# Scale vectors and normalisers loaded as rows and turned on TensorE, and the first two weight tiles sent by ScalarE

## The reference

```python
num = einsum('bhts,bhse->bhte', qk, vf) + s_in[..., None] * einsum('bhtd,bhde->bhte', qf, c)
den = sum(qk, -1) + s_in * einsum('bhtd,bhd->bht', qf, n)
h = num / maximum(abs(den), exp(-m_t))[..., None]
c_new = decay[..., None, None] * c + einsum('bhs,bhsd,bhse->bhde', wl, kf, vf)
n_new = decay[..., None] * n + einsum('bhs,bhsd->bhd', wl, kf)
```

## Time and profile before

| | |
|---|---|
| timed runs | 2895.07, 2895.27, 2896.46 us (median 2895.27) |
| profiled execution, its own time | 2887.62 us |
| its span, first to last instruction | 2885.6 us |
| TensorE busy | 2672.1 us (93%) |
| VectorE busy | 1120.3 us (39%) |
| GpSimd busy | 1074.2 us (37%) |
| ScalarE busy | 468.8 us (16%) |
| mean granted clock of TensorE | 0.961 of 2.4 GHz |
| SP's queue q1 | 255164 packets, 174.29 MB |
| ScalarE's queue q10 | 31616 packets, 15.02 MB |

### The profile page before, as it was taken

The page is one execution under the profiler, slowest core; times in us unless marked ns, Lnnn a source line. Parts: engine busy times, 40 slices in busy tenths (PEclk is TensorE's granted clock), DMA queues, the critical chain, the costliest instruction groups (busy, mean ns, idle before and its releaser), DMA issues. The chain is left out here.

```text
span 2885.6 us, 38309 instructions
## 1 busy us (share of the span) xinstructions
PE 2672.1 (93%) x15388; PEld 2605.5 (90%) x15388; DVE 1120.3 (39%) x1949; ACT 468.8 (16%) x1019; POOL 1074.2 (37%) x591
## 2 busy tenths in 40 slices
PE   7989889988999999999977968888899999999997
PEld 7978779888999999999977957788899999999996
DVE  6433343335333333333346326623533333333334
ACT  4222222212000000000013314411200000000002
POOL 1212111344444445445433420014444444455441
PEclk9999999999999999999988968989999999999998
DMA  4564766210111111111112244331111111111111
GB/s 133 148 93 131 138 140 144 70 45 30 44 44 36 44 44 39 41 44 38 42 46 64 86 110 93 85 111 40 33 44 44 38 42 44 44 43 36 44 36 73
DMA packets 287626, 190.65 MB, mean 66 GB/s; under 512 B 68196, under 2 KB 274692, under 8 KB 287516
## 3 DMA queue, kind: packets, MB, share of 16 engines
q1 hardware_dynamic: 255164, 174.29, 23.3%
q10 hardware_dynamic: 31616, 15.02, 2.1%
q0 software_dynamic: 768, 0.27, 0.0%
HBM read 148.74 MB, written 42.34 MB: 66 GB/s over the span
## 5 line engine op out<-in xcount | busy, mean ns | idle before, releaser
L233 PE MATMUL psum<-xh,wh 128*128 128x384 f32 (+1 forms) x2592 | 600.7, 340 | 53.0 <-DVE xl L199 30.2
L233 PE MATMUL psum<-xh,wl 128*128 128x384 f32 (+1 forms) x2592 | 599.6, 340 | 0.0
L233 PE MATMUL psum<-xl,wh 128*128 128x384 f32 (+1 forms) x2592 | 598.0, 339 | 0.0
L542 POOL TENSOR_TENSOR wh<-raw,ones 128x1024 fp32r<-128x1024 f32 x128 | 246.8, 1928 | 835.9 <-PE psum L233 832.7
L233 PEld LDWEIGHTS psum<-xh,wh 128*128 128x128 f32 x2592 | 469.7, 190 | 58.2 <-issue 38.6
L233 PEld LDWEIGHTS psum<-xl,wh 128*128 128x128 f32 x2592 | 470.8, 190 | 0.0
L233 PEld LDWEIGHTS psum<-xh,wl 128*128 128x128 f32 x2592 | 470.0, 189 | 0.0
L661 DVE TENSOR_TENSOR h<-h,psum 128x400 f32<-128x400 f32 (+1 forms) x528 | 262.6, 553 | 299.3 <-PE psum L233 299.3
L544 POOL TENSOR_TENSOR wl<-raw,wh 128x1024 fp32r<-128x1024 f32 x128 | 353.5, 2762 | 10.0
L1304 PE MATMUL psum<-xh,wh 128*128 128x384 f32 (+1 forms) x792 | 277.5, 350 | 7.9 <-POOL xl L1253 3.2
L1304 PE MATMUL psum<-xl,wh 128*128 128x384 f32 (+1 forms) x792 | 272.6, 344 | 0.0
(11 more groups left out here) (200 smaller groups left out, 2621.0 us busy)
## 6 DMA issues: line engine op xcount, KB each, us to landing
raw<-in_w_gate_up SPq DMA_DIRECT2D x88, 512.0 KB, 3.9
raw<-in_w_down SPq DMA_DIRECT2D x44, 512.0 KB, 3.6
raw<-in_a_w_in SPq DMA_DIRECT2D x24, 512.0 KB, 4.7
fr_qkv<-qkv_d SPq DMA_DIRECT2D x36, 256.0 KB, 4.4
qkv_d<-fr_tmp SPq DMA_DIRECT2D x32, 192.0 KB, 2.0
qr_d<-tmp ACTq DMA_DIRECT2D x8, 584.0 KB, 2.8
x_loaded<-og_d SPq DMA_DIRECT2D x8, 584.0 KB, 5.6
hn_d<-fr_hn_turned SPq DMA_DIRECT2D x36, 128.0 KB, 4.0
```

The source lines that it names most:

```text
L233: mm = pe.matmul(psum[:, bank + c, 0:nt], w(k), x[:, k, t0:t0 + nt], start=(k == 0 and n == 0), stop=(k == nk - 1 and n == 2))
L542: pool.tensor_tensor(wh[:, b, :], raw[:, r, :], unit, ALU.mult).then_inc(hi_s, 1)
```

## The change

At the start, ScalarE loads the six scale vectors as 48 rows of 128 elements, and all of `state_n` as 32 more rows, into one tile `grow`. TensorE turns the 80 rows in one transposition, and VectorE copies 48 columns into `gains` and 32 into `n_in`. ScalarE then sends weight tile 1 and the two halves of the gate tile, so that SP's stream begins with seven x tiles and the wait for tile 2.

In the mLSTM, VectorE copies a head's 8 normalisers from `n_in` into column 256 of `CS` in step 8, and after the head copies those of `CS` and `C` into `n_out`. After the last head TensorE turns `n_out` (36 columns), ScalarE copies the result into `n_rows`, and SP stores it as 32 and 4 rows of 128 elements. The loads of `state_n` and the stores of `n_s` and `n_p` in every head are gone, and the counts of the semaphores follow.

```diff
+    grow, _ = at("fr_small_rows", [6 * KD + NB * HA, P], F32, place[0] + 4 * P * 4)
     hnc = sb("hn_loaded", [P, 2, CW])
+    n_in, n_out, n_rows = sb("n_in", [P, NB, HA]), sb("n_out", [P, NB * HA + HA]), sb("n_rows", [NB * HA + HA, P])
...
-                if n >= 2:
-                    sp.wait_ge(w_hi, n - 1)
-                    sp.wait_ge(w_lo, 2 * n - 2)
-                if n == 0:
-                    sp.wait_ge(gz, 1)
-                    for half in range(2):
-                        sp.dma_start(weight_tile(raw[:, 0, :])[:, :, 32 * half:32 * half + HA],
-                                     ga[:, :, HA * half:HA * half + HA]).then_inc(w_ld[0], 16)
-                else:
-                    kind, hd, j = tiles[n]
-                    sp.dma_start(weight_tile(raw[:, n % 2, :]), (wo if kind == "out" else wi)(j)).then_inc(w_ld[n % 2], 16)
+                sp.wait_ge(w_hi, n - 1)
+                sp.wait_ge(w_lo, 2 * n - 2)
+                kind, hd, j = tiles[n]
+                sp.dma_start(weight_tile(raw[:, n % 2, :]), (wo if kind == "out" else wi)(j)).then_inc(w_ld[n % 2], 16)
...
             def load_states(hd):
                 if hd:
-                    sp.wait_ge(cs_st, 32 * hd)
+                    sp.wait_ge(cs_st, 16 * hd)
                 sp.dma_start(CS[:, :, 0:DV], a["state_c"][:, 0, hd].rearrange("b d e -> d b e")).then_inc(cs_ld, 16)
-                with nc.allow_non_contiguous_dma("normaliser columns"):
-                    sp.dma_start(CS[:, :, DV], a["state_n"][:, 0, hd].rearrange("b d -> d b")).then_inc(cs_ld, 16)
 
             def store_states(hd):
                 sp.wait_ge(csu, NB * (hd + 1))
                 sp.dma_start(a["c_s"][:, 0, hd].rearrange("b d e -> d b e"), CS[:, :, 0:DV]).then_inc(cs_st, 16)
-                with nc.allow_non_contiguous_dma("normaliser columns"):
-                    sp.dma_start(a["n_s"][:, 0, hd].rearrange("b d -> d b"), CS[:, :, DV]).then_inc(cs_st, 16)
 
             def store_c(hd):
                 sp.wait_ge(cup, 9 * (hd + 1))
                 sp.dma_start(a["c_p"][0, 0, hd], C[:, hd % 2, 0:DV]).then_inc(c_st, 16)
-                sp.dma_start(a["n_p"][0, 0, hd].rearrange("(d x) -> d x", x=1), C[:, hd % 2, DV:E1]).then_inc(c_st, 16)
...
             for i in CHUNK_X[0]:
                 load_x(i)
-            load_w(1)
-            load_w(0)
             for i in CHUNK_X[1]:
                 load_x(i)
             load_w(2)
...
+                if g == S0 + HG * HA + 1:
+                    sp.wait_ge(nrd, 1)
+                    sp.dma_start(a["n_s"].rearrange("b a h d -> (b a h) d"), n_rows[0:NB * HA, :]).then_inc(n_st, 16)
+                    sp.dma_start(a["n_p"].rearrange("b a h d -> (b a h) d"), n_rows[NB * HA:NB * HA + HA, :]).then_inc(n_st, 16)
...
             for n, g in enumerate((a["norm_mix"][0], a["a_g_head"][0], a["norm_ffn"][0], a["g_kv"],
                                    a["norm_mix"][1], a["norm_ffn"][1])):
-                with nc.allow_non_contiguous_dma("gain columns"):
-                    act.dma_start(gains[:, n, :], g.rearrange("(k p) -> p k", p=P)).then_inc(gl, 16)
+                act.dma_start(grow[KD * n:KD * n + KD, :], g.rearrange("(k p) -> k p", p=P)).then_inc(gl, 16)
+            act.dma_start(grow[6 * KD:6 * KD + NB * HA, :], a["state_n"].rearrange("b a h d -> (b a h) d")).then_inc(gl, 16)
+            act.dma_start(weight_tile(raw[:, 1, :]), wi(tiles[1][2])).then_inc(w_ld[1], 16)
+            act.wait_ge(gz, 1)
+            for half in range(2):
+                act.dma_start(weight_tile(raw[:, 0, :])[:, :, 32 * half:32 * half + HA],
+                              ga[:, :, HA * half:HA * half + HA]).then_inc(w_ld[0], 16)
...
-            act.wait_ge(gl, 96)
             w_split(0)
             x_squares(0)
             act.wait_ge(const, 5)
+            act.wait_ge(gnd, 2)
...
+                if g == S0 + HG * HA:
+                    act.wait_ge(ntd, 1)
+                    act.activation(n_rows[:], psum[0:NB * HA + HA, KB, 0:P], ACT.Copy).then_inc(nrd, 1)
...
-                    pe.wait_ge(cs_ld, 32 * (hd + 1))
+                    pe.wait_ge(cs_ld, 16 * (hd + 1))
+                    pe.wait_ge(ncd, hd + 1)
...
+            pe.wait_ge(gl, 112)
+            pe.transpose(psum[:, UB, 0:6 * KD + NB * HA], grow[:], ident[0:6 * KD + NB * HA, 0:6 * KD + NB * HA]).then_inc(grt, 1)
             turn_x(0)
...
+                if g == S0 + HG * HA:
+                    pe.wait_ge(nco, HA)
+                    pe.wait_ge(hsd, 10 * HA)
+                    pe.transpose(psum[0:NB * HA + HA, KB, 0:P], n_out[:], ident[:]).then_inc(ntd, 1)
...
-            dve.wait_ge(gl, 96)
+            dve.wait_ge(grt, 1)
+            dve.tensor_copy(gains[:].rearrange("p n k -> p (n k)"), psum[:, UB, 0:6 * KD]).then_inc(gnd, 1)
+            dve.tensor_copy(n_in[:].rearrange("p b h -> p (b h)"), psum[:, UB, 6 * KD:6 * KD + NB * HA]).then_inc(gnd, 1)
             place_x(0)
             diag(0)
+            dve.wait_ge(gnd, 2)
             x_low(0, h, 0, 0)
...
+                    if st == 8:
+                        dve.tensor_copy(CS[:, :, DV], n_in[:, :, hd]).then_inc(ncd, 1)
+                    if st == 10:
+                        dve.wait_ge(csu, NB * (hd + 1))
+                        dve.wait_ge(cup, 9 * (hd + 1))
+                        dve.tensor_copy(n_out[:, hd:NB * HA:HA], CS[:, :, DV])
+                        dve.tensor_copy(n_out[:, NB * HA + hd:NB * HA + hd + 1], C[:, hd % 2, DV:E1]).then_inc(nco, 1)
```

More of the change, by code:

```diff
@@ L815, in front @@
     rinv = sem("fr_pool_rinv")
+    grt, gnd, ncd, nco, ntd, nrd, n_st = (sem("fr_" + x) for x in (
+        "small_rows_turned", "small_columns", "n_columns", "n_collected", "n_turned", "n_rows", "n_stored"))
     qmz, vao = sem("fr_q_masked_zeroed"), sem("fr_v_ones_set")
@@ L998, in _ @@
                     sp.wait_ge(hst[1], 16 * 20)
-                    sp.wait_ge(cs_st, 32 * HA)
-                    sp.wait_ge(c_st, 32 * HA)
+                    sp.wait_ge(cs_st, 16 * HA)
+                    sp.wait_ge(c_st, 16 * HA)
                     for j in range(SPILL):
@@ L1008, in _ @@
             sp.wait_ge(meta_st, 16)
+            sp.wait_ge(n_st, 32)
             sp.wait_ge(wcopy, 32)
@@ L1482, in gated @@
                         dve.wait_ge(hst[1], 16 * 20)
-                        dve.wait_ge(cs_st, 32 * HA)
-                        dve.wait_ge(c_st, 32 * HA)
+                        dve.wait_ge(cs_st, 16 * HA)
+                        dve.wait_ge(c_st, 16 * HA)
                 dve.scalar_tensor_tensor(dst, tmp[:, g % 4, 0:nt], gains[:, 1, j:j + 1], hnc[:, k % 2, 0:nt],
@@ L1587, in state @@
                         if hd >= 2:
-                            dve.wait_ge(c_st, 32 * (hd - 1))
+                            dve.wait_ge(c_st, 16 * (hd - 1))
                         dve.tensor_copy(C[:, v, :], psum[:, UB, 0:E1]).then_inc(cup, 1)
```

## The result

The changed kernel takes 2848.4 us (median of four runs, 2842.57 to 2850.56), the kernel before beside it 2895.17 us (2894.71 to 2896.46). The ratio is 0.9835, interval 0.9818 to 0.9852: 46.8 us faster.

What follows compares the result with a forecast made beforehand. TensorE was taken as the bound, so only its waits and slow stretches pay. −35.4 + 1.0 (waits) − 1.0 (start) + 0.4 (transposition) = −35.0 us from 2887.62 gave 2852.6; with 7.65 carried over, 2860.3 us, range 2854 to 2878.

Steps and rivals of the forecast that it cites:

- the head changes: At three changes of head in the mLSTM, stalls behind the 4-byte `n_s` stores would go, gaining 35.4 us before leftover waits.
- `c_s` rivals: At the head changes, `c_s` causes half the stall (about 2878 us, chance 0.11) or all (2894.7 us, chance 0.08).
- residual waits: At the three changes of head, 1.0 us in all of waiting for loads would remain.
- new transposition: At group 66 after the last head, turning 36 collected columns on TensorE would add 0.4 us, bounds 0.3 and 1.0.
- start: At the kernel's start, the split of x would begin at 21.3 us instead of 22.28, gaining 1.0 us.
- The two rivals at the start: ScalarE's queue runs ahead of x, split near 19 us (2858 us, chance 0.04); first weights starve (above 2901 us, chance 0.03).
- After the fourth head the mLSTM steps are over and no long wait is listed, so I count nothing.: Behind the last head's `n_s` store, no stall was counted: 0 us gained there.
- I carry the same difference over.: The timed median of the kernel before lay 7.65 us above its profiled execution; the same was added for the changed kernel.

Runs made afterwards that it cites:

- third profile of before: The kernel before, run again without an edit for a trace beside its timed runs; this trace has a span of 2877.7 us and a shorter stall.
- half of `n_s`: The kernel before with 512 instead of 1024 elements in each head's `n_s` store: 2864.64 us, ratio 0.9932.
- stores only: The kernel before with only the `n_s` and `n_p` stores made as rows after the last head, start and loads as they were: 2845.28 us, ratio 0.9864.
- No `c_s`: The kernel before with the `c_s` store left out, `n_s` still stored as single elements: 2867.85 us, ratio 0.9935.

## Why the prediction was wrong

**Right: the head changes.** The sum took 35.4 us from pitches of line 1329; 35.5 went. The tenth is a match with one trace: in the third profile of before the `qkv` waits are 20.6 us, not 24.6. The cause was right as well: `n_s`, not `c_s`. That the price goes by the element was not in the forecast; half of `n_s` shows it. Both `c_s` rivals are refuted: stores only has the whole gain with `c_s` in place. No `c_s` shows what was right in them: `c_s` sets when the stall begins.

**Right within a fraction: residual waits, new transposition, start.** The 1.0 us for waits left over was about 0 (1.3 us in four waits, all under 0.5). The new transposition shows as no wait: TensorE's instruction at group 66 has no idle time before it. The start's 1.0 us became 0.7 at the split of x and 0.17 at head 0 in this trace, and 1.2 at head 0 in the mean of all. That the first split came at 16.02, near the 15.7 of the forecast, is luck: not the gate tile's landing released it, but the end of ScalarE's own issuing and the table load behind it, which the forecast had put into the wait. The two rivals at the start did not come about: the split of x was neither at 19 us nor late.

**Wrong, first: "After the fourth head the mLSTM steps are over and no long wait is listed, so I count nothing."** The fourth store cost 4 to 5.4 us. From traces: of the 41.7 us at line 233's first matmul, 5.3 come behind the last change of head; leaving out that store alone gives 5.4 in its trace and 4.1 in time. A sign of it stood in the trace of before, in VectorE's waits and not in TensorE's, which the forecast read. The lateness went from h rows to VectorE's gating, from there to GpSimd's and VectorE's splits of the output chunks, and reached TensorE 30 us later as a wait of 1.97 us and a stretch in part at 1.2 GHz.

**Wrong, second: "I carry the same difference over."** The 7.65 us between a profiled execution and a timed median were treated as a constant of the program. In four other groups the kernel before had medians 2 to 4 us below its profiled execution, with ratios of 0.9867 and 0.9861 for the changed one, about 38 to 40 us. So the change is worth some 39 us, near the 40.0 of the two profiles; in the first measurement the kernel before was 10 to 12 us slower than in the other four groups, the changed one only 2 to 5, and the difference went into the 46.8. What made it slower there stays open, since no trace of an execution of 2895 us exists.

Adding up: 36.4 (the changes of head and the 0.9 ahead of and between them) + 5.3 (the fourth store) − 1.6 (from line 233 to the end the profile after is 2252.3 − 2250.7 = 1.6 us longer) = 40.1, the difference of the spans.

## What to carry to other kernels

Price a slow transfer by what stands behind it in its queue, and follow every instance of it to the end of the kernel: where no engine waits for it at once, look in the lists of the other engines, since the lateness can reach the bounding engine much later: here it came 30 us later, as a short wait and a lower granted clock. Before 4-byte stores are spread over a kernel, gather the elements, turn them on TensorE and store rows: one transposition, a few copies and two stores cost nothing that can be told here. A difference between one profile and a few timed runs is not a term to carry: forecast the ratio of two profiles, and let the spread of repeated measurements widen the range.

## What the runs showed of the hardware

A store of 1024 single 4-byte elements holds the packets behind it in its queue for some 13 us, about 13 ns an element (an estimate from the 14 us at 41 GB/s in the earlier trace rows, the 12 us at 42 GB/s without `c_s`, and the 6.6 us that half of the elements took off a wait). The small packets are not what takes the time: in the DMA view of before, 927 of them pass from 202 to 203 us, and in the fourth store's stall, from 477 to 491 us, there are only 35 (second line). What crawls is the larger packets behind them:

```profile
DMA packets 1023, 0.14 MB, mean 141 GB/s; under 512 B 927, under 2 KB 1023, under 8 KB 1023
...
DMA packets 695, 0.57 MB, mean 40 GB/s; under 512 B 35, under 2 KB 695, under 8 KB 695
```

The loads of `state_n`, also by 4 bytes, have no such effect: from 114 to 117 us of before 1103 packets under 512 bytes pass, and the mean is 303 GB/s. The Trainium skill, page "DMA: Bandwidth & Descriptors", section "Specifications", says that below 512 bytes the DMA engine does a read-modify-write. That the stores of 4 bytes are dear agrees with it; the read-modify-write itself is in no run, and for the loads none shows a price. The Trainium skill, same page, section "Queues, rings and completion order", says that a semaphore's increment lands only after every earlier write of the same engine, which would make later loads seem late; the traces show more than that, since the packets themselves are spread out at 41 GB/s.

The layout of the target may count: after the last head, 1024 elements into one block of 4 KB landed in 13.7 us, into eight rows that lie apart in 19.2. That is one store against one, in two kernels that differ in more. The 128 elements of `n_p` hold their queue on a small scale. In the kernel before, and then in stores only, this is the DMA view at the head of `c_s` (195 to 199 us, and 193 to 197.5):

```profile
DMA packets 120, 0.08 MB, mean 20 GB/s; under 512 B 12, under 2 KB 120, under 8 KB 120
```

```profile
DMA packets 1661, 1.44 MB, mean 319 GB/s; under 512 B 55, under 2 KB 1661, under 8 KB 1661
```

With `n_p` as columns 0.08 MB pass in 4 us, without it 1.44 MB in 4.5. This costs no time by itself: the run without `n_s` has the whole gain with `n_p` still stored by columns.
